# Reordering the side work of a hybrid decoder layer: attention of block B ahead of the recurrence's second half

## Chip, cores and metric

One core of a Trainium2 chip. The metric is the device time of one execution, in microseconds (us). TensorE is PE in the profile (PEld its weight loads), VectorE DVE, ScalarE ACT, GpSimd POOL, SyncE SP.

## What is computed

One layer of a decoder with two groups of heads, over 1024 prompt tokens and 8 sample tokens (each the next token of its own running sequence). Cut to what matters:

```python
def hybrid_layer(x, p, gla_fn, attn_fn, lambda_init):
    z = rmsnorm(x, p['norm_mix_g']) @ p['w_in']          # gq gk gv gg glr dq dk dv, 3088 columns
    log_a = log_sigmoid(glr @ p['w_gk2'] + p['b_gk']) / 16
    S_new, o_g = gla_fn(q_g, k_g, v_g, log_a)            # S_t = diag(a_t) S_{t-1} + k_t^T v_t, o_t = q_t S_t
    o_g = rmsnorm(o_g, p['gla_norm_g']) * silu(gg)
    o_d = attn_fn(rmsnorm(dq), rmsnorm(dk), dv, lam)     # softmax(q1 k1^T) - lam softmax(q2 k2^T), times v
    o_d = rmsnorm(o_d, p['diff_norm_g']) * (1.0 - lambda_init)
    x = x + concat(o_g, o_d) @ p['w_out']
    u = square(relu(rmsnorm(x, p['norm_ffn_g']) @ p['w_up']))
    return x + u @ p['w_down'], k_d, v_d, S_new
```

The prompt goes through the recurrence from a zero state and through causal attention. Each sample token has a state of its own and attends to 2048 cached positions (16 pages of 128, named by a page table) and to itself. All is fp32; the dense products are three fp32r matmuls each, of high and low parts (lines 85 to 87).

## The kernel before

**Blocks and the main line.** The tokens are two blocks: A, 512 tokens, and B, 512 and the 8 sample tokens. The main line of all engines is: `front` (the input projections, group by group: gv, low, gk, gq, dq, dk, dv, gg), then `feed_forward` for A, then for B. A feed forward is 8 output tiles of the mixing product ("out"), then 8 groups of 4 "up" tiles and 8 "down" tiles. Each weight tile is loaded by SP, split by ACT (high, L1982 and L1997) and DVE (low, L1986 and L2074). Block A's feed forward takes its results from two PSUM banks in turn; DVE frees one by an add (L2104, L2143) or by the scaled relu (L2125).

**Ticks.** The main line is cut into ticks of 12 dense matmuls: 104 in the front, 144 in a feed forward (an out or up tile is 2 ticks, a down tile 1). At each tick every engine calls the side jobs that `program` has put there by hand (`put(name, ticks)`) and each takes one step: a Python generator that issues a few instructions for that engine and yields. So the order within each engine's queue is fixed by this table; between engines only semaphores order. SP, which issues all DMAs, waits in its queue too.

**Side jobs of before** (ticks of the front by their number, of A's feed forward from 0): recurrence A (`recurA`), front; `attnA`, 40 steps at two a tick from front tick 79; `keysA`, front ticks 73 to 103; `mixA` from 96. Beside A's feed forward: `recurB` 0 to 34, `keysB` 0 to 66, `attnB` 33 to 72, `soft` 66 to 73, `values` 73 to 143, `sgla` 77 to 101 at every second, `mixload` 126, `mixB` from 137.

**The jobs.** `recurrence`: 4 chunks of 128 tokens, 8 steps each: subtract (DVE, L1114, L1116), exponentials (ACT, L1206 to L1209), keys and queries times decay (DVE, L1134 into `kp`, L1139 into `e`), then at the chunk's fifth step PE: transpose (L1254), levels (L1238), and later the products with values. `attention`: 16 units (4 heads, 4 query tiles), two steps each: scores on PE (L1412, L1415), maxima (DVE, L1537 or L1540), exponentials (ACT, L1468), mix of the two softmaxes (DVE, L1546 to L1548), transposes (PE, L1429), copies (ACT, L1478), product with the values (PE, L1443), its square and copy (ACT, L1482, L1488), the root of the head norm (POOL, L1519 to L1524), the scaling (ACT, L1493). `cached_keys`: per page a load of 256 KB, a product with the sample's query spread over the partitions (POOL, L2238), a reduction (DVE, L2226); block A's half of the 128 pages has 3 buffers and one for the query, B's half 4 and 2. `sample_softmax` works on all scores of the cached keys; `cached_values` loads two pages a step and multiplies them by coefficients laid out in `a_pad` (PE, L2443), after masks made by POOL (L2378 to L2382). `sample_recurrence` (`sgla`) updates the 8 states (PE, L2497; DVE, L2546) and reads them (PE, L2505). `mixing` turns the rows of both head groups for the mixing product (PE, L1640; DVE, L1663).

Buffers are given by hand at fixed places of SBUF, so a job that takes over a place first waits for the last reader (`region_free`, `sample_free`).

## Time and profile before

| | us |
|---|---|
| three runs | 1630.32, 1639.47, 1637.55 (median 1637.55) |
| profiled execution: time, span | 1636.6, 1634.7 |
| PE busy | 1465.6 (90%) |
| PE weight loads busy | 1182.6 (72%) |
| DVE busy | 852.0 (52%) |
| ACT busy | 531.1 (32%) |
| POOL busy | 316.6 (19%) |
| feed forward of A, first to last dense matmul | 491 to 1191 |
| feed forward of B | from 1192 |

The span is from the first to the last instruction; the execution's own time has some 2 us around it. A busy PE is not a PE at its peak: matmuls of 512 columns overlap, and their told length depends on the granted clock. Idle time before an instruction is put down to what ended it.

### The profile page before, as it was taken

Reading aid. Unit: us, or ns where it says so; the run is one execution under the profiler, and the core shown is the slowest. Engines: PE = TensorE matmul, PEld = TensorE weight load, DVE = VectorE, ACT = ScalarE, POOL = GpSimd, SP = SyncE. Lnnn points to the kernel's source line nnn. Section 1 sums busy time; section 2 is a strip of 40 time slices with the busy share of each in tenths; the row PEclk is TensorE's granted clock in tenths of the full one; section 3 lists DMA queues with packets and bytes.
Section 4 is the critical chain, followed back from the end, with each engine's and each line's share of the span. In section 5 each row is a group of like instructions: output and inputs, shape, how many; then the busy total and the mean of one; then the engine's idle time right before and its main releaser. Section 6 shows DMA issues by size and latency. Waiting matters only on the chain.

```text
span 1634.7 us, 23191 instructions
## 1 busy us (share of the span) xinstructions
PE 1465.6 (90%) x8649; PEld 1182.6 (72%) x8649; DVE 852.0 (52%) x1326; ACT 531.1 (32%) x964; POOL 316.6 (19%) x366
## 2 busy tenths in 40 slices
PE   7999988967778858789898999999989999999998
PEld 5787767745556646567676566565679999999998
DVE  4353565444556778565766433343435455554442
ACT  5462332223323342244543111121224233333222
POOL 2201222354563433233331000000012000000000
PEclk9999989978888878899998999999999999999999
DMA  7532231553345533534323556566423222322121
GB/s 247 157 98 87 59 100 59 177 153 109 116 147 175 178 126 123 196 99 130 123 90 109 181 174 189 178 221 218 141 93 129 103 103 104 104 104 91 66 77 54
DMA packets 115634, 211.99 MB, mean 130 GB/s; under 512 B 12665, under 2 KB 45722, under 8 KB 115522
## 3 DMA queue, kind: packets, MB, share of 16 engines
q1 hardware_dynamic: 115522, 210.50, 40.2%
q8 instruction: 69, 1.13, 0.3%
q14 instruction: 43, 0.35, 0.1%
HBM read 184.00 MB, written 26.46 MB: 129 GB/s over the span
## 4 chain that ended last, share of the span: by engine, by line
PE 56%; DVE 9%; ACT 4%; issue 3%; DMA 2%; POOL 2%; SPq 0%; ACTq 0%; POOLq 0%; DVEq 0%
PE ps L85 16%; PE ps L86 15%; PE ps L87 15%; PE ps L2443 4%; DVE uw_l L1986 2%; PE ps L1412 2%; POOL kr L2238 1%; PE ps L1238 1%; DMA kr<-in_cache_k 1%; ACT uw_h L1982 1%; DVE e L1114 1%; PE ps L1443 1%; DVE sd L2226 1%; DVE stat L1540 1%; DVE e L1139 1%
## 5 line engine op out<-in xcount | busy, mean ns | idle before, releaser
L85 PE MATMUL ps<-uh,dh 128*128 128x512 f32 (+2 forms) x768 | 253.9, 331 | 7.7 <-DVE xt L2143 7.7
L87 PE MATMUL ps<-uh,dl 128*128 128x512 f32 (+2 forms) x768 | 248.1, 323 | 0.0
L86 PE MATMUL ps<-ul,dh 128*128 128x512 f32 (+2 forms) x768 | 247.9, 323 | 0.0
L2238 POOL TENSOR_TENSOR kr<-kr,qb 128x512 f32<-128x512 f32 x128 | 174.8, 1375 | 160.1 <-DMA kr<-in_cache_k 119.7
L2143 DVE TENSOR_TENSOR xt<-xt,ps 128x256 f32<-128x256 f32 (+2 forms) x192 | 97.2, 511 | 179.8 <-PE ps L87 179.0
L85 PEld LDWEIGHTS ps<-uh,dh 128*128 128x128 f32 x768 | 146.4, 191 | 39.1 <-DVE xt L2143 19.8
L1982 ACT ACTIVATE uw_h<-raw_up 128x1024 fp32r<-128x1024 f32 x80 | 84.4, 1056 | 246.5 <-PE ps L87 246.5
L87 PEld LDWEIGHTS ps<-uh,dl 128*128 128x128 f32 x768 | 146.2, 190 | 12.1
L86 PEld LDWEIGHTS ps<-ul,dh 128*128 128x128 f32 x768 | 146.3, 191 | 9.8
L1997 ACT ACTIVATE dh<-raw_dn 128x1024 fp32r<-128x1024 f32 x64 | 67.0, 1047 | 261.2 <-PE ps L87 260.5
L85 PE MATMUL ps<-x2hB,uw_h 128*128 128x264 f32 (+1 forms) x512 | 145.9, 285 | 3.2 <-DVE uw_l L1986 2.6
L86 PE MATMUL ps<-x2lB,uw_h 128*128 128x264 f32 (+1 forms) x512 | 145.5, 284 | 0.0
L87 PE MATMUL ps<-x2hB,uw_l 128*128 128x264 f32 (+1 forms) x512 | 145.3, 284 | 0.0
L2226 DVE TENSOR_REDUCE sd<-kr 128x8 f32<-128x512 f32 x128 | 86.8, 679 | 79.3 <-POOL kr L2238 78.9
L1986 DVE TENSOR_TENSOR uw_l<-raw_up,uw_h 128x1024 fp32r<-128x1024 f32 x80 | 100.0, 1250 | 49.6 <-ACT uw_h L1982 49.6
L85 PE MATMUL ps<-x2hA,uw_h 128*128 128x512 f32 x256 | 110.9, 433 | 9.8 <-DVE uw_l L1986 9.8
L2125 DVE SCALAR_TENSOR_TENSOR xr<-ps,rb 128x256 f32<-128x256 f32 (+1 forms) x96 | 49.1, 514 | 116.1 <-PE ps L87 115.7
L86 PE MATMUL ps<-x2lA,uw_h 128*128 128x512 f32 x256 | 104.0, 406 | 0.0
L87 PE MATMUL ps<-x2hA,uw_l 128*128 128x512 f32 x256 | 103.6, 405 | 0.0
L2074 DVE TENSOR_TENSOR dl<-raw_dn,dh 128x1024 fp32r<-128x1024 f32 x64 | 81.2, 1268 | 37.7 <-ACT dh L1997 37.4
L85 PEld LDWEIGHTS ps<-x2hB,uw_h 128*128 128x128 f32 x512 | 97.3, 190 | 3.7 <-DVE uw_l L1986 2.8
L86 PEld LDWEIGHTS ps<-x2lB,uw_h 128*128 128x128 f32 x512 | 97.2, 190 | 0.0
(324 smaller groups left out, 2948.7 us busy)
## 6 DMA issues: line engine op xcount, KB each, us to landing
kr<-in_cache_k SPq DMA_DIRECT2D x128, 256.0 KB, 3.0
raw_up<-in_w_up_units SPq DMA_DIRECT2D x64, 512.0 KB, 3.7
raw_dn<-in_w_down SPq DMA_DIRECT2D x64, 512.0 KB, 4.6
vr<-in_cache_v SPq DMA_DIRECT2D x128, 256.0 KB, 3.1
raw<-in_w_in_units SPq DMA_DIRECT2D x24, 512.0 KB, 4.1
raw_up<-in_w_out_units SPq DMA_DIRECT2D x16, 512.0 KB, 3.8
xin<-in_x_prompt SPq DMA_DIRECT2D x8, 512.0 KB, 5.5
xt_scratch<-xts SPq DMA_DIRECT2D x8, 512.0 KB, 5.9
```

The source lines that it names most:

```text
L85: pe.matmul(out, lh, rh, start=first and n == 0, stop=False)
L86: pe.matmul(out, lh, rl, start=False, stop=False)
L87: ins = pe.matmul(out, ll, rh, start=False, stop=last and n == len(ks) - 1)
L1982: act.activation(uw_h[:, t % 2, :, :], raw_up[:, t % 2, :].rearrange("p (k c) -> p k c", c=P), ACT.Copy).then_inc(up_high, 1)
L1986: dve.tensor_tensor(uw_l[:, t % 2, :, :], raw_up[:, t % 2, :].rearrange("p (k c) -> p k c", c=P), uw_h[:, t % 2, :, :].bitcast(FP32), ALU. ...
L1997: act.activation(dh[:, x, :], raw_dn[:, x % 2, :], ACT.Copy).then_inc(dn_high, 1)
L2074: dve.tensor_tensor(dl[:, x, :], raw_dn[:, x % 2, :], dh[:, x, :].bitcast(FP32), ALU.subtract).then_inc(dn_low, 1)
L2125: dve.scalar_tensor_tensor(vt[:, i % 2, 0:spans[p][1]], ps[:, bank("up", g, x, p), 0:spans[p][1]], 0.0, rb2[:, tokens(p)], ALU.max, ALU.mu ...
L2143: dve.tensor_tensor(xt[:, o, c], xt[:, o, c], ps[:, bank("down", g, o, p), 0:spans[p][1]], ALU.add).then_inc(added, 1)
L2226: dve.tensor_reduce(m["sd"][:, b, g, :], ring[v % n_ring][:, :].rearrange("p (h d) -> p h d", d=DH), X, ALU.add).then_inc(k_used, 1)
L2238: pool.tensor_tensor(k[:, :], k[:, :], qb[b % len(qb)][:, :], ALU.mult).then_inc(k_multiplied, 1)
L2443: ins = pe.matmul(ps[32 * g:32 * g + 32, 6 + b % 2, :], a_pad[:, b % 2, 2 * l + j, :], vring[v % VRING][:, j, :], start=l < 2, stop=l >= 6 ...
```

## The change

The side jobs of A's feed forward stand in another order: `attnB` at ticks 0 to 42 (not at 17, in which the feed forward's norm uses a bank of the attention), 20 pages of `keysB` beside it at every second tick, the other 44 in ticks 43 to 68 with `sgla` at every second of 44 to 68, `soft` 68 to 75, `values` 75 to 143, `recurB` 71 to 105, `mixload` 108. The loads of `attnB` start in front tick 101. Cached keys have one query buffer, and 4 page buffers in block A, 3 and then 6 in block B; in block A the reduction comes a step later. The recurrence's keys and queries share one tile, `e`, and only the half of each level that is read is multiplied. In attention the root and the scaling come one step later. Banks and places change with it: values and softmax use banks 2 and 3, `sgla` 4 to 6, mixing B four banks; gg's tiles take the two banks in the other order. POOL fills `a_pad` and the mask once the coefficients are made, as `a_pad` takes the place of the scores. Cut to its core:

```diff
-        return g % 3 if GROUPS[g][0] not in ("dv", "gg") else GROUPS[g][1] % 2
+        kind, x = GROUPS[g]
+        return g % 3 if kind not in ("dv", "gg") else (x + (kind == "gg")) % 2
...
-            act.activation(tq[:, x % 2, :], ps[:, x % 2, :], ACT.Tanh, scale=m["hr"][:, x:x + 1]).then_inc(gate_soft, 1)
+            act.activation(tq[:, x % 2, :], ps[:, bank_of(START["gg"] + x), :], ACT.Tanh, scale=m["hr"][:, x:x + 1]).then_inc(gate_soft, 1)
...
-    g_in = at(f"g_in{part}", 166.625, [P, 3, 2, P])
-    gv = at(f"gv_in{part}", 169.625, [P, W])
-    e = at(f"e{part}", 171.625, [P, 9, 2, P])
-    kp = at(f"kp{part}", 180.625, [P, 8, 2, P])
-    at_sb = at(f"at_sb{part}", 188.625, [P, H, P])
-    kd = at(f"kd{part}", 190.625, [P, 2 * P])
+    base = (166.625, 178.625)[part]
+    g_in = at(f"g_in{part}", base, [P, 3, 2, P])
+    gv = at(f"gv_in{part}", base + 3, [P, W])
+    e = at(f"e{part}", base + 5, [P, 9, 2, P])
+    at_sb = at(f"at_sb{part}", base + 14, [P, H, P])
+    kd = at(f"kd{part}", base + 16, [P, 2 * P])
-    go = at(f"go{part}", 193.625, [P, W])
-    gate = at("gate1", 195.625, [P, W]) if part else None
+    go = at("go1", base + 17, [P, W]) if part else None
+    gate = at("gate1", base + 19, [P, W]) if part else None
...
-            eng.wait_ge(sem("product_made"), UNITS)
-            eng.wait_ge(sem("exped"), 2 * UNITS)
-            eng.wait_ge(sem("od_made"), UNITS)
-            eng.wait_ge(sem("mix_turned"), 8)
-            eng.wait_ge(sem("k_used"), KEY_PAGES)
+            eng.wait_ge(sem("product_made"), 2 * UNITS)
+            eng.wait_ge(sem("os_done"), 1)
+            eng.wait_ge(sem("state_stored"), 16)
...
+                dve.wait_ge(kd_turned, c)
...
-            dve.tensor_tensor(kp[:, :, :, :], e[:, 1:9, :, :], g_in[:, 1, :, :].unsqueeze(1).to_broadcast([P, 8, 2, P]),
-                              ALU.mult).then_inc(kq_made, 1)
+            k = g_in[:, 1, :, :]
+            dve.tensor_tensor(e[:, 8, :, :], e[:, 8, :, :], k, ALU.mult)
+            for l in range(1, 8):
+                v = side_of(e[:, l, :, :], l, 0)
+                ins = dve.tensor_tensor(v, v, side_of(k, l, 0), ALU.mult)
+            ins.then_inc(kq_made, 1)
...
-            dve.tensor_tensor(e[:, 0:8, :, :], e[:, 0:8, :, :], g_in[:, 0, :, :].unsqueeze(1).to_broadcast([P, 8, 2, P]),
-                              ALU.mult).then_inc(kq_made, 1)
+            q = g_in[:, 0, :, :]
+            dve.tensor_tensor(e[:, 0, :, :], e[:, 0, :, :], q, ALU.mult)
+            for l in range(1, 8):
+                v = side_of(e[:, l, :, :], l, 1)
+                ins = dve.tensor_tensor(v, v, side_of(q, l, 1), ALU.mult)
+            ins.then_inc(kq_made, 1)
...
-                        lhs = g_in[r, 1, t, :] if l == 0 else kp[r, l - 1, t, :]
+                        lhs = g_in[r, 1, t, :] if l == 0 else e[r, l, t, :]
...
-            pe.wait_ge(sem("exped"), 2 * UNITS)
-            pe.wait_ge(sem("p_copied"), UNITS)
-            pe.wait_ge(sem("od_made"), UNITS)
+            m["attend_banks_free"](pe)
+            pe.wait_ge(sem("os_done"), 1)
...
-ATTEND_STEPS = 2 * (UNITS + 4)
+ATTEND_STEPS = 2 * (UNITS + 5)
...
-        for x in ("o_summed", "state_summed", "s_updated", "go_made"):
-            eng.wait_ge(sem(x), CHUNKS * (part + 1))
-        if part:
-            eng.wait_ge(sem("og_gated"), NTILE)
-            eng.wait_ge(sem("go_out"), 64)
+        if part == 0:
+            for x in ("o_summed", "state_summed", "s_updated", "go_made"):
+                eng.wait_ge(sem(x), CHUNKS)
+        else:
+            eng.wait_ge(sem("product_made"), UNITS)
+            eng.wait_ge(sem("mix_turned"), 8)
+            eng.wait_ge(sem("k_used"), KEY_PAGES)
...
-        for x in ("o_summed", "state_summed", "go_made"):
-            sp.wait_ge(sem(x), CHUNKS * (part + 1))
-        sp.wait_ge(sem("level_picked"), 8 * CHUNKS * (part + 1))
-        m["kq_stored"](sp)
+        if part == 0:
+            for x in ("o_summed", "state_summed", "go_made"):
+                sp.wait_ge(sem(x), CHUNKS)
+            sp.wait_ge(sem("level_picked"), 8 * CHUNKS)
+            m["kq_stored"](sp)
+        else:
+            sp.wait_ge(sem("product_made"), UNITS)
         load_scored(sp, 0)
         load_scored(sp, 1)
         yield
         m["v_stored"](sp, part)
+        if part:
+            sp.wait_ge(sem("mix_turned"), 8)
         load_values(sp, 0)
...
-                pe.wait_ge(sem("rb2_made"), 1)
-                pe.wait_ge(sem("level_picked"), 8 * NTILE)
+                pe.wait_ge(sem("exped"), 2 * UNITS)
...
+            if part and n == NORM_UNIT and j == 1:
+                pe.wait_ge(sem("norm_step"), 1)
...
-                if 0 <= n - 4 < UNITS:
-                    normed(n - 4)
                 if 0 <= n - 3 < UNITS:
                     square(n - 3)
             else:
                 if 0 <= n - 2 < UNITS:
                     copy_turned(n - 2, 1)
+                if 0 <= n - 4 < UNITS:
+                    normed(n - 4)
             yield
 
...
-            u = n - 3
-            if j == 1 and 0 <= u < UNITS:
+            u = n - 4
+            if j == 0 and 0 <= u < UNITS:
...
-MIX_RING = 6
+MIX_RING = 8
+
+NORM_UNIT = 6
...
-        rowsB = at("rowsB", 192.625, [P, MIX_RING, W])
+        rowsB = at("rowsB", 178.625, [P, MIX_RING, W])
...
-    BANKS = 2 if part else 4
+    BANK0, BANKS = 2 + 2 * part, 4
...
-        return 7 - p if part else 2
+        return 7 - p if part else 6
...
-                pe.wait_ge(sem("mix_low"), 8)
+                pe.wait_ge(sem("p_copied"), UNITS + 2 * NORM_UNIT + 1)
...
+KEY_SLOTS = ((204.6875, 162.6875, 184.6875, 164.6875), (202.6875, 204.6875, 162.6875),
+             (166.625, 168.625, 170.625, 172.625, 174.625, 176.625))
+KEYS_BESIDE = 20
+
+
+def key_slots(v):
+
+    n = v - KEY_PAGES
+    return (0, 0) if n < 0 else (1, KEY_PAGES) if n < KEYS_BESIDE else (2, KEY_PAGES + KEYS_BESIDE)
...
+    LAG = 4 - part
+    STEPS = KEY_PAGES + LAG
...
+            if n:
+                sp.wait_ge(k_multiplied, PAGES * n)
+            sp.dma_start(qb[:, :], a["zq"][n].partition_broadcast(P)).then_inc(qb_in, 16)
...
+            v = first + s - 1
...
+            if s == 1 and part:
+                sp.wait_ge(sem("mix_turned"), 8)
+                sp.wait_ge(sem("k_used"), first)
+                load_query(0)
+            if first <= v < first + KEY_PAGES:
+                same = [x for x in range(v) if key_sem(x) == key_sem(v)]
+                if same:
+                    sp.wait_ge(k_used, same[-1] + 1)
+                if v == KEY_PAGES + KEYS_BESIDE:
+                    sp.wait_ge(sem("product_made"), 2 * UNITS)
+                page = sp.value_load(m["pages"][0:1, v:v + 1], min_val=0, max_val=NPOOL - 1)
+                sp.dma_start(place(v)[:, :], a["cache_k"][bass.ds(page, 1), :, :].rearrange("a p n -> p (a n)"))\
+                    .then_inc(page_in[key_sem(v)], 16)
+            n = s - 2
+            if n > 0 and n % PAGES == 0 and n < KEY_PAGES:
+                load_query(n // PAGES)
...
+            v = first + s - LAG
...
-    a_pad = at("a_pad", 182.625, [P, 2, PAGES, 32])
-    hmask = at("hmask", 186.625, [P, W])
-    vm = at("vm", 188.625, [P, W])
+    a_pad = at("a_pad", 9.75, [P, 2, PAGES, 32])
+    hmask = at("hmask", 1.5, [P, W])
+    vm = at("vm", 162.6875, [P, W])
...
+        sp.wait_ge(sem("product_made"), 2 * UNITS)
+        sp.wait_ge(sem("k_used"), 2 * KEY_PAGES)
...
-        pool.wait_ge(sem("p_turned"), 3 * UNITS)
+        pool.wait_ge(sem("coef_made"), 1)
+        pool.wait_ge(sem("k_multiplied"), 2 * KEY_PAGES)
...
-                        pe.wait_ge(v_masked, b - 1)
+                        pe.wait_ge(v_added, b)
...
-                    ins = pe.matmul(ps[32 * g:32 * g + 32, 6 + b % 2, :], a_pad[:, b % 2, 2 * l + j, :],
+                    ins = pe.matmul(ps[32 * g:32 * g + 32, 2 + b % 2, :], a_pad[:, b % 2, 2 * l + j, :],
...
-    st_new = at("st_new", 192.625, [P, NS, 2, P])
+    st_new = at("st_new", 178.625, [P, NS, 2, P])
...
-                    ins = pe.matmul(ps[:, 2 + x % 2, t * 2 * DV:(t + 1) * 2 * DV], k_alone[x // 4][:, x % 4, t * P:(t + 1) * P],
+                    ins = pe.matmul(ps[:, 5 + x % 2, t * 2 * DV:(t + 1) * 2 * DV], k_alone[x // 4][:, x % 4, t * P:(t + 1) * P],
...
-        put("keysA", [t0 + 31 * i // (KEY_PAGES + 3) for i in range(KEY_PAGES + 3)])
+        put("keysA", [t0 + 31 * i // (KEY_PAGES + 4) for i in range(KEY_PAGES + 4)])
         t0 = TICK[START["gg"]]
+        put("loadB", [t0 + 14])
         put("mixA", [t0 + 9, t0 + 10, t0 + 11, t0 + 12] + [t0 + 13 + i // 2 for i in range(7)])
         t0 = FRONT_TICKS
-        put("recurB", range(t0, t0 + side["recurB"]["steps"]))
-        t1 = t0 + side["recurB"]["steps"] - 2
-        put("loadB", [t1, t1 + 2])
-        put("attnB", [t1] + [t1 + 1 + i for i in range(ATTEND_STEPS - 1)])
-        put("keysB", range(t0, t0 + KEY_PAGES + 3))
-        t1 += 33
+        put("loadB", [t0 + 1])
+        norm = 2 * KT + 1
+        put("attnB", [t0 + i for i in range(ATTEND_STEPS + 1) if i != norm])
+        late = t0 + ATTEND_STEPS + 1
+        put("keysB", [t0 + 2 * (i + 1) for i in range(KEYS_BESIDE)])
+        put("keysB", [late + 25 * i // (KEY_PAGES + 3 - KEYS_BESIDE) for i in range(KEY_PAGES + 3 - KEYS_BESIDE)])
+        put("sgla", range(late + 1, late + 1 + 26, 2))
+        t1 = late + 25
         put("soft", [t1 + i for i in (0, 1, 3, 4, 5, 6, 7)])
         put("values", range(t1 + 7, t0 + FEED_TICKS))
-        put("sgla", range(t1 + 11, t1 + 11 + 26, 2))
-        put("mixload", [t0 + 126])
+        put("recurB", range(t1 + 3, t1 + 3 + side["recurB"]["steps"]))
+        put("mixload", [t1 + 40])
         put("mixB", [t0 + 137 + i // 2 for i in range(9)])
 
         def run(e, eng):
...
-            for name in ("attnB", "soft", "sgla", "values", "mixB"):
+            for name in ("values", "mixB"):
```

Left out are further places of tiles and bank numbers of the same kinds.

## Rows read from the trace of the kernel before

**Rows 1.** Stretches: length; busy us of PE, PEld, DVE, ACT, POOL; clock; DMA share, GB/s.

```profile
320.00:491.00 171.00, 120.05 (x544) 86.68 (x544) 86.05 (x149) 54.12 (x172) 95.52 (x107) 0.84 0.44 131
491.00:670.00 179.00, 140.49 (x771) 112.40 (x772) 131.74 (x185) 57.60 (x94) 67.14 (x48) 0.85 0.45 144
670.00:865.00 195.00, 168.19 (x866) 126.02 (x865) 130.71 (x174) 85.90 (x188) 64.19 (x76) 0.95 0.39 126
865.00:898.00 33.00, 26.30 (x107) 20.78 (x106) 18.59 (x30) 11.06 (x23) 6.00 (x11) 0.84 0.42 134
898.00:1192.00 294.00, 291.15 (x1239) 176.95 (x1237) 119.75 (x167) 56.76 (x74) 2.54 (x4) 0.99 0.57 181
```

**Rows 2.** Timeline of PE, 472 to 481: start, length, instruction.

```profile
473.15 0.63 PE L85 MATMUL ps<-wh,xhB 128*128 128x512 f32 x1
473.58 0.63 PE L86 MATMUL ps<-wl,xhB 128*128 128x512 f32 x1
...
480.63 0.39 PE L86 MATMUL ps<-wl,xhB 128*128 128x512 f32 x1
480.86 0.40 PE L87 MATMUL ps<-wh,xlB 128*128 128x512 f32 x1
```

**Rows 3.** Groups by line, 320 to 491: count, busy us, mean ns, idle before.

```profile
L2238 POOL TENSOR_TENSOR kr<-kr,qb 128x512 f32<-128x512 f32 x59 | 74.6, 1277 | 37.0 <-DMA kr<-in_cache_k 36.8
L2226 DVE TENSOR_REDUCE sd<-kr 128x8 f32<-128x512 f32 x59 | 40.4, 684 | 65.5 <-POOL kr L2238 65.3
...
L86 PE MATMUL ps<-wl,xhB 128*128 128x512 f32 x56 | 24.5, 437 | 0.0
```

**Rows 4.** Waits, 320 to 491: who for whom, us in total, times, longest.

```profile
DVE sd L2226 <- POOL kr L2238: 65.3, 39, 4.9
POOL oss L1522 <- ACT ps L1482: 36.9, 13, 8.1
...
PE ps L1443 <- ACT od L1488: 17.8, 7, 5.4
...
PE ps L85 <- DVE zs L769: 10.8, 1, 10.8
```

**Rows 5.** Waits, 491 to 670.

```profile
PE ps L1238 <- DVE e L1139: 16.5, 3, 8.1
...
PE ps L85 <- DVE uw_l L1986: 11.3, 2, 9.8
...
PE ps L1254 <- DVE kp L1134: 4.7, 3, 2.7
```

**Rows 6.** Timeline of DVE, 627 to 637.

```profile
629.75 5.66 DVE L1114 TENSOR_TENSOR e<-g_in 128x256 f32<-128x256 f32 x7
635.33 0.41 DVE L1116 TENSOR_TENSOR e<-g_in 128x256 f32<-128x256 f32 x1
```

**Rows 7.** Waits, 670 to 865.

```profile
PE ps L1429 <- ACT attn_t L1478: 12.6, 6, 3.3
...
PE ps L1412 <- DMA qt<-kept_qt: 5.9, 1, 5.9
```

**Rows 8.** The chain that ended last, 670 to 865: attention B's first and last scores.

```profile
678.64 2.51 PE ps L1412 x8
...
844.80 1.92 PE ps L1412 x8
```

**Rows 9.** Groups by line, 670 to 865.

```profile
L1986 DVE TENSOR_TENSOR uw_l<-raw_up,uw_h 128x1024 fp32r<-128x1024 f32 x10 | 13.9, 1394 | 8.5 <-ACT uw_h L1982 8.5
```

**Rows 10.** Groups by line, 898 to 1192.

```profile
L1986 DVE TENSOR_TENSOR uw_l<-raw_up,uw_h 128x1024 fp32r<-128x1024 f32 x16 | 19.6, 1225 | 5.8 <-ACT uw_h L1982 5.8
...
L2497 PE MATMUL ps<-zs,k_alone 8*128 8x256 f32 x32 | 8.0, 387 | 0.0
L2505 PE MATMUL ps<-st_new,q 128*8 128x128 f32 x64 | 7.2, 272 | 0.0
```

**Rows 11.** Timeline of POOL, 871 to 880.

```profile
875.80 3.32 POOL L2382 TENSOR_SCALAR_AFFINE_SELECT hmask<-hmask 128x512 f32<-128x512 f32 x4
```

More of the change, by code:

```diff
@@ L1605, in load @@
         for u in range(MIX_RING):
-            load_unit_rows(sp, u)
+            t, half = tiles[u]
+            sp.dma_start(rowsB[:, u, :], a[("og", "od_scratch")[half]][HALF + t * P:HALF + (t + 1) * P, :])\
+                .then_inc(b_in, 16)
         yield
-    def load_unit_rows(sp, u):
-        t, half = tiles[u]
-        sp.dma_start(rowsB[:, u % MIX_RING, :], a[("og", "od_scratch")[half]][HALF + t * P:HALF + (t + 1) * P, :])\
-            .then_inc(b_in[u // MIX_RING], 16)
-    def sync(sp):
-        for s in range(STEPS):
-            if part and s == 3:
-                for u in range(MIX_RING, 8):
-                    sp.wait_ge(turned, before + u - MIX_RING + 1)
-                    load_unit_rows(sp, u)
-            yield
     def tensor(pe):
@@ new lines, in sync @@
+            if s == 1 and part == 0:
+                last_scale(sp)
+                sp.wait_ge(sem("kv_stored"), 32)
+                m["kq_stored"](sp)
+                for x in ("o_summed", "state_summed", "s_updated", "go_made"):
+                    sp.wait_ge(sem(x), CHUNKS)
+                load_query(0)
+            if s == 1 and part:
[11 more added lines that the diff above has]
+                    .then_inc(page_in[key_sem(v)], 16)
```

171 lines of the change are left out of this document (77 added, 94 removed).

## The prediction

> **What bounds the kernel now.** I read the stretches first, then who waits for whom in each. The PE row of the page hides what matters here: its 90% is a mean over stretches with different limits [rows 1]. From 898 to 1192, with the cached values beside the feed forward, PE is busy 291.2 of 294 us: nothing can be won there but PE work itself. In the four stretches before it, PE idles 51.0, 38.5, 26.8 and 6.7 us, together 123. After an idle stretch matmuls run at half clock for a while: a 512-column matmul then starts 0.43 us after the last, against 0.23 at full clock, and is told as 0.63 us long against 0.39 [rows 2]. A mean of 437 ns [rows 3] says that a fifth ran at half clock from 320 to 491; of the 264 dense ones that is some 55 times 0.2 = 11 us. I spread this by the granted clock (0.16, 0.15, 0.05 and 0.16 below full, times the length of each stretch): 11, 11, 4 and 2, together 28 us. So some 150 us between 320 and 898 are neither PE work nor speed. The PE instructions of the change are the ones of before in another order, so only these 150 can move. The sum below is against the profiled execution, 1636.6 us (span 1634.7), 1 us under the median.
>
> The unit of the schedule, a tick, is 12 dense matmuls: 12 times 0.23 = 2.8 us at full clock. The feed forward has 144.
>
> **Front, 320 to 491.** PE waits there for ACT's copy of attention A's result and for a sample row of the projection [rows 4]. Both stand behind one knot: DVE idles 65.3 us in 39 waits for POOL's key products; POOL idles 36.9 for ACT's square [rows 4] and 36.8 for pages [rows 3]; ACT is fed by DVE. The change touches it in four places: a fourth page buffer; one more step between POOL and DVE (LAG 4); the roots one step later on POOL, the scaling one on ACT; gg's banks swapped, so that its first tile takes the bank that came free a tile earlier. A page takes 171/59 = 2.9 us now; four buffers for three make 2.2 of that if the round trip is all of it, and POOL's own floor is 1.28 [rows 3]. The three query reloads stay. The sample row's 10.8 I take down to 4, since what is left is DVE's own backlog; the other 40 of idle I take to about 22, and clock with them (11 to 6). Of 62 I keep 32: **-30**. Bounds: -45 if only POOL's floor held, -10 if only the bank swap counted.
>
> **Recurrence B.** It sat beside the first 35 ticks; there PE waits 16.5 and 4.7 us for its products and 11.3 for low weights, most of it at the feed forward's norm [rows 5]. Its chain (subtract, exp, keys, queries) lasts longer than the four ticks of 2.8 us that it is given. One set of seven subtractions takes 5.66 us with POOL beside it, where one alone takes 0.41 [rows 6]. It moves beside the values: 294 us for 70 ticks, 4.2 a tick, DVE busy 120 and POOL 2.5 [rows 1]. The four chunks waited 21 plus some 6 of slow clock; I keep 5: **-22**. Its narrower products (8 instructions for 1, half the columns) I cost at **-3** for the eight chunks; +3 if each small one carries more overhead than it saves. The added wait for the keys' transpose is over long before. Queued behind recurrence B's waits on SP is the values' loading; the state that it waits for was sent 7 ticks before, some 20 us.
>
> **Attention B** moves from ticks 33-72 to 0-42. Its scores waited 5.9 for qt, its turned blocks 12.6 for ACT's copies [rows 7]. Its first loads, 1.5 MB, now go out in the front's last ticks beside key pages (hidden by them; +4 there if not): -6. Its pace was (844.80 - 678.64)/15 = 11.1 us a unit [rows 8], of which 5.7 is dense work. An up tile has two weight splits of 1.22 on DVE [rows 10] and two half as wide, some 3.8 us; an out tile one less, 3. So I take the same pace, with fewer keys beside it: -3. The norm, for which attention leaves out tick 17, no longer stands behind a set of subtractions: -5. The sample row before the first out tile: -3, as that tile takes the other bank. Together **-17**.
>
> **Keys B.** 20 pages beside attention, then 44 in 25 ticks with the sample recurrence: 25 times 2.8, and 8.0 + 7.2 us of that recurrence's PE work [rows 10], is 85 us. POOL needs 44 times 1.28 [rows 3] = 56 and two query reloads that nothing hides now, 4 to 5 each: 66, below 85, with six buffers. On DVE an up tile has its 3.8 and 3.8 pages at 0.68 [rows 3], 6.4 for 5.7 of PE, and the sample recurrence's adds. I take **+10** (0 if the down ticks catch it up, +28 by the first rival).
>
> **Softmax, fill, mixing.** The softmax keeps its 6.7 of idle [rows 1]. New: POOL clears a_pad and builds hmask only after the coefficients; the last part alone is 3.32 us [rows 11], the whole some 5. DVE waits for it at its first value step, and its adds for the down tiles are queued behind; PE's two banks cover 5.6. The recurrence's first chunk stands in that queue too: **+6**. Mixing B has four banks for two (-2), but the sample result is due two ticks later (+3): **+1**.
>
> **Sum:** -30 -22 -3 -17 +10 +6 +1 = -55, so 1581.6; the recurrence A chain before 320 may give 1.5 more beside the stretches read here: **1580**.
>
> **A rule weighed.** The row first: DVE's split of weights takes 1394 ns with POOL busy a third of the time [rows 9], and 1225 with it idle [rows 10], 0.17 us more on the mean. The Trainium skill (SBUF — State Buffer, section SBUF: two separate sides) says that a GpSimd instruction and a VectorE one with two SBUF inputs take turns at a shared port pair, each for its whole length. Rows 6, 9 and 10 agree in direction; no row shows how often they meet.
>
> **Rivals.**
> 1. *Keys stay at the front's pace* (20%). SP issues pages in order behind the weights. At 2.9 us a page 44 take 128 us, where I have 95: +33, less what the down ticks catch up, some +28: **1608**. For: the waits of rows 4. Against: six buffers, and no roots beside.
> 2. *Exclusive turns* (8%). If pages and DVE's two-input instructions never overlapped, an up tile would need 3.8 times 1.28 plus 3.1 (two splits at 1.22, one of 0.65) = 8.0 us for 5.7. Six such tiles: +14: **1594**. For: the 5.66 of rows 6. Against: only 1394 for 1225. This is what the Trainium skill's rule on the port pair would do here, held to the letter.
> 3. *Attention loses its cover* (9%), slower than before. It now starts with the out tiles, whose banks DVE frees by an add; in DVE's queue stands the mix, which waits for ACT, which waits for PE's turned block. In its stretch a unit has 7.4 us of DVE's time and 4.9 of ACT's (130.7 and 85.9 over 17.6 units [rows 1]); with all of it behind the 5.7 of dense work a unit would take 18, with most of it 16, for 11. Place: the units from tick 1 to the second down phase, 13: +65: **1645**. Over all sixteen it decides from 57/16 = 3.6 us a unit on.
> 4. *Nothing moves* (8%). Each wait taken away is taken over by the next in DVE's queue, which has nearly the same work in it: **1637**, give or take 6.
>
> **How the numbers follow.** Forecast 55%, rivals 20, 8, 9 and 8. A measurement here tells about 0.5% (8 us) from no change. Forecast and rivals 1 and 2 end faster, 0.83, less 0.01 for rival 1's upper end; same 0.09, slower 0.09. Range: down to the front at -45, the keys at 0 and ten more from the waits of attention B (1545); up past rival 1 to where rival 4 begins (1622). It leaves out rivals 3 and 4 and a little more.
>
> **What would show it.** Right: DVE's wait for POOL's keys in the front under 35 us; no wait of PE over 3 us for the recurrence's queries; attention's scores 11 us apart or less; the keys' 25 ticks within 100 us; a granted clock of 0.9 or more from 320 on. Wrong: DVE waits for POOL in the keys' ticks (rival 1), weight splits of 1.6 us and more (rival 2), PE waits for ACT's copies or for DVE's adds in the out ticks (rival 3). The forecast fails as a whole if the front's stretch stays over 160 us.

## The result, and the profile after

The changed kernel takes 1594.2 us (median of 4 runs, 1590.33 to 1599.75), the kernel before 1636.98 in the same comparison: a ratio of 0.9747, 95% interval 0.9703 to 0.9792. That is 43 us less; 57 were forecast, and the range (1545 to 1622) holds the result. The profiled execution of after is the longest of its four (1599.75, span 1598.0), which matters below.

Stretches of the changed kernel, cut where its stages end (columns as in [rows 1]):

```profile
320.00:457.00 137.00, 107.46 (x526) 77.94 (x526) 87.58 (x144) 52.88 (x169) 88.83 (x103) 0.94 0.49 151
457.00:678.00 221.00, 199.19 (x992) 150.39 (x991) 138.40 (x174) 105.69 (x223) 62.60 (x76) 0.94 0.38 128
678.00:795.00 117.00, 95.55 (x401) 73.94 (x400) 76.99 (x106) 17.08 (x21) 62.48 (x44) 0.88 0.51 167
795.00:842.00 47.00, 28.68 (x95) 22.00 (x94) 31.94 (x58) 13.96 (x16) 2.69 (x4) 0.75 0.31 112
842.00:1151.00 309.00, 302.51 (x1495) 190.08 (x1493) 150.68 (x277) 73.97 (x118) 10.09 (x15) 0.99 0.55 180
```

The stages are: 320 the front's end, 457 attention B with 20 key pages, 678 the other 44 pages with the sample recurrence, 795 the softmax, 842 cached values with the recurrence's second half, 1151 block B's feed forward. PE idles 29.5, 21.8, 21.5, 18.3 and 6.5 us in the five from 320 to 1151, 98 in all; it was 126 from 320 to 1192 [rows 1]. A's feed forward starts at 457.3, where it started at 491.1. That is no fair mark, since PE waits for the sample row right before 491.1 in the kernel before (6.2 us) and behind its first tick in this one (4.5). By the start of the third tick, 498.8 before and 471.0 now, 28 us are won. From there to its last matmul it takes 679.6 us for 692.3: 13 more. Behind it the profiled execution gives 4 back (447.4 for 443.6).

The waits of the changed kernel in the front, which answer to the knot of [rows 4], DVE's and then PE's (us in total, times, longest):

```profile
DVE sd L2265 <- POOL kr L2277: 21.5, 17, 3.4
```

```profile
PE ps L1466 <- ACT od L1511: 15.2, 7, 6.5
...
PE ps L1450 <- DVE p0a L1571: 5.7, 3, 4.2
PE ps L85 <- DVE wl L729: 1.9, 1, 1.9
```

DVE's wait for POOL's key products fell from 65.3 us in 39 to 21.5 in 17, and the 10.8 for the sample row is gone (1.9, for something else). The wait for ACT's copy of attention A's result is nearly what it was, 15.2 for 17.8.

The waits of all engines in the key ticks, 678 to 795, the stage that did not do as forecast:

```profile
POOL kr L2277 <- DMA kr<-in_cache_k: 25.4, 11, 7.1
POOL kr L2277 <- DMA qb<-kept_zq: 18.0, 2, 14.5
...
DVE sd L2265 <- POOL kr L2277: 15.3, 10, 5.5
...
PE ps L85 <- DVE xt L2159: 10.6, 1, 10.6
...
PE ps L85 <- DVE dl L2090: 6.5, 1, 6.5
...
PE ps L2539 <- DVE st_new L2588: 4.3, 1, 4.3
```

Behind them stand two places. First, DVE's timeline around 694 (start, us, instruction, how many):

```profile
694.03 3.43 DVE L2566 TENSOR_TENSOR k_alone<-kq_g,ident 8x1024 f32<-8x1024 f32 x2
697.39 4.89 DVE L2573 COPY q<-gbs 64x8 f32<-64x8 f32 x4
702.31 0.69 DVE L2159 TENSOR_TENSOR xt<-xt,ps 128x512 f32<-128x512 f32 x1
```

The four copies L2573 move 8 numbers a partition, 0.17 us each in the kernel before (0.155 to 0.173), and take 1.2 each here; PE's 10.6 us end with the add behind them, at 702.3. POOL multiplies eight pages without a pause meanwhile, and the single records go in step: the copies end at 698.61, 699.84, 701.06 and 702.28, each 0.03 us after the end of a page's product (698.59, 699.81, 701.03, 702.25). Second, from 709 POOL stands still; POOL's timeline, then SP's issues, and what SP waited for between 700 and 726:

```profile
690.43 11.82 POOL L2277 TENSOR_TENSOR kr<-kr,qb 128x512 f32<-128x512 f32 x8 [3.17 <-DMA kr<-in_cache_k]
...
723.81 2.48 POOL L2277 TENSOR_TENSOR kr<-kr,qb 128x512 f32<-128x512 f32 x2 [14.51 <-DMA qb<-kept_zq]
```

```profile
704.34 1.45 SPq L2252 DMA_DIRECT2D kr<-in_cache_k  x2
717.22 0.34 SPq L1793 DMA_DIRECT2D raw_up<-in_w_up_units  x1
717.61 0.43 SPq L1805 DMA_DIRECT2D raw_dn<-in_w_down  x1
719.13 0.36 SPq L2252 DMA_DIRECT2D kr<-in_cache_k  x1
719.54 0.42 SPq L2230 DMA_DIRECT2D qb<-kept_zq  x1
720.74 1.46 SPq L2252 DMA_DIRECT2D kr<-in_cache_k  x2
```

```profile
SPq L1793 <- DVE uw_l L2002: 11.4, 1, 11.4
```

The page multiplied at 723.8 needed the next sample's query row. SP sent its load only at 719.5: in SP's queue it stood behind two weight loads (717.2, 717.6) whose buffers had to come free. PE's waits in the other stages, 457 to 678, 795 to 842 and 842 to 1151:

```profile
PE ps L1450 <- ACT attn_t L1501: 9.5, 6, 2.7
PE ps L85 <- DVE zs L770: 4.5, 1, 4.5
PE ps L1429 <- ACT p1b L1491: 3.3, 1, 3.3
```

```profile
PE ps L2301 <- DVE small L2332: 9.0, 1, 9.0
PE ps L2309 <- DVE small L2349: 6.0, 1, 6.0
PE ps L2305 <- DVE small L2338: 3.3, 1, 3.3
```

```profile
PE ps L85 <- DVE xt L2159: 6.3, 1, 6.3
```

No wait of PE for a product of the recurrence's second half is left: in the old first ticks it had 21.2 us [rows 5]. What is left of its cost is the 6.3 us just shown: before that add, DVE waits 4.0 us for ACT's part of a weight split, which stands behind two of the recurrence's exponentials of 1.9 us each. The softmax has 18.3 of PE's waits for three DVE results, where the kernel before had 6.5 in the softmax's ticks and 2.7 for attention's copy.

### The profile page after: what moved, and what is told of

The parts are those of the page before. It is cut to its first block, busy times and chain, and to the rows that moved or that the text cites. A ratio compares the mean times of both kernels' runs of the same rounds, so it can differ in the third digit from the quotient of the medians.

```text
span 1598.0 us, 23302 instructions
## 1 busy us (share of the span) xinstructions
PE 1456.0 (91%) x8649; PEld 1176.5 (74%) x8649; DVE 850.0 (53%) x1438; ACT 530.1 (33%) x964; POOL 313.9 (20%) x366
## 4 chain that ended last, share of the span: by engine, by line
PE 55%; DVE 8%; issue 5%; DMA 3%; ACT 3%; POOL 2%; SPq 1%; ACTq 0%; POOLq 0%; DVEq 0%
PE ps L85 16%; PE ps L87 15%; PE ps L86 15%; PE ps L2486 4%; DMA kr<-in_cache_k 2%; POOL kr L2277 1%; PE ps L1429 1%; DVE uw_l L2002 1%; PE ps L1250 1%; PE ps L1466 1%; DVE sd L2265 1%; ACT uw_h L1998 1%; DMA out_y_prompt<-y 1%; PE ps L1450 1%; DVE stat L1563 1%
## 5 line engine op out<-in xcount | busy, mean ns | idle before, releaser
L2277 POOL TENSOR_TENSOR kr<-kr,qb 128x512 f32<-128x512 f32 x128 | 170.7, 1354 | 151.1 <-DMA kr<-in_cache_k 104.6
L86 PE MATMUL ps<-x2lB,uw_h 128*128 128x264 f32 (+1 forms) x512 | 144.7, 283 | 0.0
L85 PE MATMUL ps<-x2hA,uw_h 128*128 128x512 f32 x256 | 111.1, 434 | 10.6 <-DVE xt L2159 10.6
```

Source lines behind the costliest of these rows:

```text
L85: pe.matmul(out, lh, rh, start=first and n == 0, stop=False)
L86: pe.matmul(out, lh, rl, start=False, stop=False)
L2277: pool.tensor_tensor(k[:, :], k[:, :], qb[:, :], ALU.mult).then_inc(k_multiplied, 1)
```

## The experiments

All ratios are to the kernel before, with their 95% intervals. The changed kernel stands at 0.9747. A difference of two ratios times 1637 is what one kernel has over another. Most intervals are 4 us to either side, the changed kernel's is 7: a difference to the changed kernel is uncertain by some 8 us, one between two others by some 6. So a small difference rests on what the traces show beside it. A wait "in tick 47" lies between that tick's twelve matmuls and the next tick's first.

**What made the front's gain.** Three runs undo one part of the changed kernel each; one makes the front's edits, all but the roots', on the kernel before.

e1_bank:

```diff
     def bank_of(g):
         kind, x = GROUPS[g]
-        return g % 3 if kind not in ("dv", "gg") else (x + (kind == "gg")) % 2
+        return g % 3 if kind not in ("dv", "gg") else x % 2
```

> The changed kernel with the bank swap of the gate tiles undone (gg's first tile again takes the bank of dv's last). Theory 1, each repair of the front has its own share: PE's wait of about 10.9 us for the first gate tile comes back (it is 1.9 in the changed kernel), the time goes from 1594 to about 1602, ratio to before 0.979. Theory 2, it was only DVE's backlog and the wait moves elsewhere: ratio 0.975, within 2 us of 1594, and the waits of the other tiles shrink by as much.

Measured: 1599.59 us, ratio 0.9761 (0.9738 to 0.9785): 2 us more by the ratios, 5 by the medians. PE's waits for the sample row, from 320 to 480:

```profile
PE ps L85 <- DVE zs L770: 16.5, 2, 8.4
```

The sample row's wait is back, 16.5 us in two: 8.4 in the front, and 8.1 right before the feed forward's first matmul, where the changed kernel has 4.5 a tick later. By the third tick it is 4.5 us behind the changed kernel (475.5 for 471.0), and by the ninth 4.4. So the swap is worth 2 to 5 us, under half of the 12 us of waits that it takes away: between the two theories.

e2_slots3:

```diff
-KEY_SLOTS = ((204.6875, 162.6875, 184.6875, 164.6875), ...
+KEY_SLOTS = ((204.6875, 162.6875, 184.6875), ...
...
-    LAG = 4 - part
+    LAG = 3
...
-        put("keysA", [t0 + 31 * i // (KEY_PAGES + 4) for i in range(KEY_PAGES + 4)])
+        put("keysA", [t0 + 31 * i // (KEY_PAGES + 3) for i in range(KEY_PAGES + 3)])
```

> The changed kernel with block A's cached keys back at three buffers and three steps between load and sum. Theory 1 (the page's round trip held the front, what the prediction leaned on): DVE's wait for POOL's key products in the front goes from 21.5 us back to 50 or more, the front loses 15 to 25 us, time about 1614, ratio 0.986. Theory 2 (it was the roots' order on POOL): DVE's wait rises by less than 15 us, time under 1600, ratio 0.977.

Measured: 1610.77 us, ratio 0.984 (0.9816 to 0.9863), 15 us more; the third tick starts at 487.6, 16.6 later. DVE's waits for POOL in its front:

```profile
DVE sd L2265 <- POOL kr L2277: 41.8, 26, 4.9
```

41.8 us of waits for POOL against 21.5: under the 50 that I had put for theory 1, but the time is theory 1's, at its lower end. The fourth buffer with its longer distance is the largest single part; which of these two carries it was not run apart.

e3_roots puts POOL's root and ACT's scaling back to one step earlier (the later stages keep their ticks); POOL's part of the edit:

```diff
-            u = n - 4
-            if j == 0 and 0 <= u < UNITS:
+            u = n - 3
+            if j == 1 and 0 <= u < UNITS:
                 x, e, total = oss[:, u % 4:u % 4 + 1], stat[:, u % 4, 7:8], stat[:, u % 4, 0:1]
```

> The changed kernel with attention's roots on POOL and the scaling on ACT back at one step earlier (the places of the later stages are kept). Theory 1 (the buffers alone made the gain): POOL's wait for ACT's square comes back (37 us in the front before) but PE hardly sees it, time within 3 us of 1594, ratio 0.975 to 0.977. Theory 2 (POOL's in-order wait for the square held the key products behind it, and DVE behind them): DVE's wait for POOL in the front rises from 21.5 to over 40 us, time 1602 to 1612, ratio 0.98 to 0.985.

Measured: 1596.22 us, ratio 0.9745 (0.9719 to 0.9771), no difference. POOL's wait for ACT's square comes back at 16.5 us, not at 36.9, and DVE's waits for POOL stay at 23.4. The third tick even starts 4.2 us earlier (466.8), but attention B's ticks 8 to 42 take 181.2 us for 174.8. Theory 1 held: this part of the change, which I had counted among four, carries nothing that these runs can tell. The edit puts both blocks' attention back, and in its trace the two places pull against each other.

b2_front, on the kernel before: the bank swap, the fourth buffer and LAG 4 as above, with block A's attention moved by 64 bytes to make room.

> The kernel before with the front's edits alone, without the roots' step: the fourth page buffer of block A's keys, one more step to DVE, and gg's banks swapped. Theory 1 (the front's gain stands by itself): the feed forward starts 30 to 38 us earlier than 491, the time is 1600 to 1606, ratio 0.978 to 0.981, so that the rest of the change brings only some 10. Theory 2 (the gain needs the later stages, or is given back at the feed forward's start): the front ends 30 us earlier but the time falls by under 20, ratio over 0.988.

Measured: 1607.55 us, ratio 0.9813 (0.9789 to 0.9837), 31 us less than before. The third tick starts at 464.1, 34.7 earlier, and 5 of that are gone by the ninth (502.0 for 531.5): between them PE waits 5.4 us for recurrence B and 3.5 for a low weight split. So the front's gain stands by itself, and all the rest of the change, with six jobs moved, brings 11 by the ratios, 13 by the medians, give or take 8. The parts that e1_bank and e2_slots3 undo come to 17 to 20 us of the front's 28 to 31; the rest needs the swap and the buffers together, or is noise, and no run tells which.

**The narrower products.** b1_narrow, on the kernel before:

```diff
-            dve.tensor_tensor(e[:, 0:8, :, :], e[:, 0:8, :, :], g_in[:, 0, :, :].unsqueeze(1).to_broadcast([P, 8, 2, P]),
-                              ALU.mult).then_inc(kq_made, 1)
+            q = g_in[:, 0, :, :]
+            dve.tensor_tensor(e[:, 0, :, :], e[:, 0, :, :], q, ALU.mult)
+            for l in range(1, 8):
+                v = side_of(e[:, l, :, :], l, 1)
+                ins = dve.tensor_tensor(v, v, side_of(q, l, 1), ALU.mult)
+            ins.then_inc(kq_made, 1)
```

(and the keys in the same way, into `e` instead of `kp`)

> The kernel before with nothing but the narrower products of the recurrence (the multiplied keys written over e, eight instructions of half the columns for one wide one). Theory 1 (the prediction's term of 3 us for eight chunks): 1634, ratio 0.998. Theory 2 (each product is shorter by 0.4 to 1.4 us as in the changed kernel, and in the first 320 us and from 491 to 590 PE waits for them, so it is worth more): 8 to 10 us, ratio 0.994 to 0.995. Theory 3 (hidden): 1.000.

Measured: 1636.45 us over 12 runs, ratio 0.999 (0.9974 to 1.0005): 1.6 us less, 4.3 less to 0.8 more. Theory 1's 3 us are within that, and so is theory 3's nothing; theory 2's 8 to 10 are not. In the changed kernel a set of narrow products takes 1.83 us all eight times, where the wide one took 2.28 to 3.35. In this run thirteen of the sixteen sets do so too, but three of the four query sets beside the feed forward take 3.96, 5.04 and 5.13 us, longer than the wide products that they replace (2.28, 3.35 and 2.75). The second of these three, DVE's timeline and then POOL's:

```profile
602.25 1.49 DVE L1149 TENSOR_TENSOR e<-e,g_in 128x256 f32<-128x256 f32 x1
603.66 3.63 DVE L1152 TENSOR_TENSOR e<-e,g_in 128x128 f32<-128x128 f32 x7
```

```profile
601.99 4.14 POOL L2251 TENSOR_TENSOR kr<-kr,qb 128x512 f32<-128x512 f32 x3 [23.52 <-DMA qb<-kept_zq]
```

POOL's three products end at 603.45, 604.86 and 606.12, and three of DVE's eight end 0.15 to 0.29 us later (603.73, 605.00, 606.27), at 1.35 to 1.49 us each; the others take 0.28. In the fourth query set, at 507, it is POOL's page that takes 3.89 us, and DVE's eight take their 1.83. PE's waits in the first stage beside the feed forward:

```profile
PE ps L1251 <- DVE e L1152: 18.1, 3, 8.9
PE ps L85 <- DVE uw_l L1999: 12.9, 3, 9.8
```

18.1 us, where 16.5 stood: cutting one product into eight shortens a set by 0.4 us and more where POOL leaves it alone, and lengthened three by 1.7 to 2.4 where pages come in turn with its pieces. So this run prices the narrow products in the old order. In the changed kernel, where recurrence B stands beside a POOL that is all but idle, no run has them apart.

**Why the rest brought only 11.** e4_query starts from the changed kernel; each later one says from which.

e4_query, a second buffer for the query row of the third sample of the late pages (block B had two query buffers before the change):

```diff
+    qb6 = at("qb6", 162.6875, [P, W]) if part else None
...
-            if n:
+            if n == 6:
+                sp.wait_ge(k_used, 82)
+            elif n == 7:
+                sp.wait_ge(k_multiplied, 97)
+            elif n:
                 sp.wait_ge(k_multiplied, PAGES * n)
...
-            if n > 0 and n % PAGES == 0 and n < KEY_PAGES:
+            if n > 0 and n % PAGES == 0 and n < KEY_PAGES and not (part and n > PAGES):
                 load_query(n // PAGES)
+            if v in (84, 100):
+                load_query(2 if v == 84 else 3)
```

> The changed kernel with a second buffer for block B's third query row, so that the last two query loads are sent 12 pages ahead instead of when POOL needs them. Theory 1 (the 14.5 us of idle on POOL at 709 to 724, behind SP's weight loads, cost PE its waits of 4.3 and 6.5 us and more in the ticks 50 to 58): the gap falls under 4 us, the 25 key ticks from 116.7 to about 108, time 1586, ratio 0.970. Theory 2 (DVE's own work in these ticks is the bound, and POOL only catches up): the gap goes, the 25 ticks stay at 114 or more, time 1593, ratio 0.974.

Measured: 1586.84 us, ratio 0.9697 (0.9668 to 0.9725), 8 us less than the changed kernel; the 25 key ticks take 108.6 us for 116.7. PE's waits in them:

```profile
PE ps L85 <- DVE xt L2159: 10.9, 1, 10.9
PE ps L85 <- DVE dl L2090: 8.3, 1, 8.3
```

Theory 1: the wait of 4.3 us for the state's adds is gone, and so is POOL's 14.5 for a query. It also shows how one execution differs from the next: attention's ticks 0 to 42, in which nothing differs, take 214.0 us for 220.9, at a granted clock of 0.98 for 0.94 in that stretch. The ratios and medians are what the 8 us go by, and they are no more than their uncertainty; what bears them out is that the key ticks take 114.6 to 116.7 us in all four traces without this edit (the changed kernel's, e1_bank, e2_slots3, e3_roots).

e5_q4act, e4_query with the four small copies on ACT:

```diff
-                st.note(dve.tensor_copy(diag, gbs[r, 0, t, :]))
...
+        act.wait_ge(k_alone_made, 2)
+        for t in range(2):
+            for hf in range(2):
+                r = rows[hf]
+                diag = q4[:, :, :, :, :].rearrange("p t h b c -> p t h (b c)")[r, t, hf, 0:64:9]
+                act.activation(diag, gbs[r, 0, t, :], ACT.Copy).then_inc(sem("gbs_made"), 1)
```

> The kernel of e4_query with the sample recurrence's four small copies of queries (8 elements a partition each) moved from DVE to ACT. On DVE they took 4.89 us for four while POOL multiplied eight pages without a pause, 0.76 in the kernel before. Theory 1 (DVE's small copies each wait for a whole POOL page, and this delays the add that PE waits for 10.9 us at in tick 47): on ACT the four take under 1.5 us beside the same pages, PE's wait there falls to about 6, time 1582 to 1583, ratio to e4_query 0.997. Theory 2 (the copies are slow on any engine, from their strided output): they take 4 us or more on ACT too.

Measured: 1585.92 us, ratio 0.9691 (0.9668 to 0.9713). By itself 1 us is no difference, and theory 1's time is missed by 3. In its trace, though, PE's wait in tick 47 falls from 10.9 to 6.1 us and the key ticks from 108.6 to 104.6, as theory 1 has it; e10_both below tries the copies once more. ACT's timeline, and POOL's at the same time:

```profile
690.80 0.93 ACT L2539 ACTIVATE q<-gbs 64x8 f32<-64x8 f32 x4 [22.09 <-DVE k_alone L2584]
```

```profile
683.75 17.41 POOL L2287 TENSOR_TENSOR kr<-kr,qb 128x512 f32<-128x512 f32 x10 [3.05 <-DMA kr<-in_cache_k]
```

Four copies in 0.93 us on ACT beside a POOL that runs on, 4.89 on DVE. The copies are not slow in themselves: it is DVE beside POOL. With the ends in step shown above this is the exclusive turn of my second rival, at an instruction that I had not thought of. The Trainium skill (SBUF — State Buffer, section Who interferes with whom) lists VectorE's copy among the operations that can take the port pair shared with GpSimd, and says that the second one then waits for the whole instruction of the first; 1.2 us a copy beside products of 1.26 us agrees. The same section says that on trn2 a reduction never meets it, and DVE's reductions of the pages did take 0.67 to 0.69 us in all 128 places, beside POOL as elsewhere.

e6_lag, e4_query with the late pages loaded a step earlier ahead of POOL, and summed two steps behind it:

```diff
-    LAG = 4 - part
-    STEPS = KEY_PAGES + LAG
+    LATE = KEY_PAGES + KEYS_BESIDE
+    STEPS = KEY_PAGES + (5 if part else 4)
+
+    def made_at(v):
+        return v - first + (2 if v < LATE else 3)
+
+    def summed_at(v):
+        return v - first + (4 if part == 0 else 3 if v < LATE else 5)
```

> The kernel of e4_query with a longer distance for the late pages of block B's keys: POOL multiplies two steps after SP sends the load instead of one, DVE sums two steps after that instead of one. Theory 1 (SP's order behind the weight loads makes pages late, and DVE in its turn waits 8.5 us in 8 for POOL and is then late for the split that PE waits 8.3 us for in tick 55): DVE's waits fall under 3 us, PE's wait in tick 55 under 3, time 1580 to 1582. Theory 2 (the bound is DVE's own work, four sums and four state adds in front of the split): the wait of tick 55 stays over 6 us, time within 2 us of e4_query's 1586.8.

Measured: 1578.78 us, ratio 0.9651 (0.9626 to 0.9676), 7.5 us less than e4_query; the key ticks take 101.4. PE's waits in them, then DVE's:

```profile
PE ps L85 <- DVE dl L2090: 5.8, 1, 5.8
PE ps L85 <- DVE xt L2159: 4.8, 1, 4.8
```

```profile
DVE sd L2280 <- POOL kr L2291: 0.8, 2, 0.5
```

The time and DVE's waits (8.5 to 0.8) are theory 1's. The wait for the split in tick 55 fell only from 8.3 to 5.8, not under 3, so part of it is DVE's own work, as theory 2 has it. The wait in tick 47 fell from 10.9 to 4.8, although the four copies take 4.92 us there too: the sums in front of them no longer wait for pages. The edit moves two distances at once. POOL's own waits for pages hardly change (34.5 us in 15 in e4_query, 32.5 in 17 here), so what its 7.5 us buy is that DVE no longer stands behind a late page; what the earlier load alone would bring was not run.

e10_both, e6_lag with e5_q4act's copies (the base that the next three are read against):

> The kernel of e6_lag with e5_q4act's copies on ACT and nothing else: the base of e7_soft, which had both and the respaced softmax. The key ticks took 101.4 us in e6_lag and 97.1 in e7_soft. Theory 1 (the copies are worth their 4 us also here, and the respaced softmax gave its part back): about 1575, ratio 0.9625 to 0.963, and the key ticks 97 to 98 us. Theory 2 (they are hidden once the pages come late, and the spacing neither gained nor lost): 1578 to 1580, ratio 0.965, the key ticks over 100 us.

Measured: 1575.09 us over 6 runs, ratio 0.961 (0.9583 to 0.9637), under e6_lag by 4 us by the medians and 7 by the ratios; the key ticks take 96.1 for 101.4. That stretch, and PE's waits in it:

```profile
678.00:774.00 96.00, 90.58 (x400) 70.31 (x399) 72.98 (x102) 18.13 (x25) 66.80 (x45) 0.95 0.65 206
```

```profile
PE ps L85 <- DVE dl L2090: 3.9, 1, 3.9
PE ps L2560 <- DVE st_new L2605: 1.5, 1, 1.5
```

Theory 1. The wait of tick 47 is gone altogether. This is the fastest kernel of the study, 19 us under the changed one by the medians and 22 by the ratios, outside both intervals; its PE idles 5.4 us in the key ticks against 21.4.

e7_soft, e10_both with the softmax spaced out:

```diff
-        put("soft", [t1 + i for i in (0, 1, 3, 4, 5, 6, 7)])
-        put("values", range(t1 + 7, t0 + FEED_TICKS))
+        put("soft", [t1 + i for i in (0, 3, 5, 6, 8, 9, 10)])
+        put("values", sorted(list(range(t1 + 11, t0 + FEED_TICKS)) + [t0 + i for i in (93, 109, 125)]))
```

> The kernel of e6_lag with e5_q4act's copies on ACT, and the softmax of the cached scores given ten ticks for seven (its PE steps three, two and three ticks behind the DVE steps they need, the values' steps start four ticks later and catch up by three doubled steps in down ticks). Theory 1 (PE's three waits of 7.2, 3.3 and 7.3 us in ticks 69, 71 and 73 come from PE being sent there before DVE's queue can be done): they fall under 6 us in sum, 10 to 12 us less; with 1 us for the copies the time is 1566 to 1569, ratio 0.958. Theory 2 (DVE's queue in these ticks is itself the bound and the waits reappear as waits for its splits or adds): under 4 us less, 1575 or more.

Measured: 1579.87 us, ratio 0.9658 (0.9634 to 0.9682), slower than e10_both by 8 us by the ratios and 5 by the medians (their intervals overlap by 0.0003). PE's waits in the softmax's ticks, and from there to the end:

```profile
PE ps L2319 <- DVE small L2352: 6.6, 1, 6.6
PE ps L85 <- DVE dl L2090: 4.4, 1, 4.4
PE ps L85 <- DVE uw_l L2002: 2.1, 1, 2.1
PE ps L2323 <- DVE small L2363: 1.3, 1, 1.3
```

```profile
PE ps L2487 <- DVE vm L2479: 5.0, 1, 5.0
PE ps L1656 <- DVE zs L2472: 4.7, 1, 4.7
...
PE ps L2500 <- DMA vr<-in_cache_v: 2.3, 1, 2.3
```

17.8 us of softmax waits became 7.9, as theory 1 wanted, and 6.5 us of waits for DVE's splits are new; then the values' doubled steps make PE wait for a page (2.3) and for the mask's product (5.0), and the sample's result comes later into block B's mix (4.7 for 1.9). The feed forward takes 670.2 us for e10_both's 670.4, the part behind it 450.7 for 445.3. Theory 2 has the time (over 1575), and part of the place: 6.5 us reappear as waits for splits. The rest went to the far end, which neither theory had.

e8_rec, e7_soft with `recurB` at t1 + 12 and `mixload` at t1 + 49:

> The kernel of e7_soft with the recurrence's second half started nine ticks later, behind the softmax, where in the changed kernel its first chunk's subtractions, exponentials and products stand in DVE's queue during the softmax (about 7 us of DVE). Theory 1 (the first chunk in the queue costs PE what the prediction put down, some 3 of its 6 us): 3 to 4 us less than e7_soft. Theory 2 (after the spacing DVE has the time): within 1.5 us of e7_soft. Theory 3 (its end meets the mix of block B): slower by 2 us or more.

Measured: 1578.31 us, ratio 0.9645 (0.9617 to 0.9672), within 2 us of e7_soft, which can't be told from theory 1's 3 to 4 or theory 2's 1.5. The softmax's eleven ticks 68 to 78 fall from 58.9 to 41.3 us, and the 29 after them rise from 144.7 to 157.6, the last 36 from 149.8 to 152.7: the work is moved, not hidden. In those 29 PE waits 8.9 us for DVE's adds and 5.9 for loads of values, where e7_soft has 3.1 and 2.3 from its softmax on.

e9_even, e8_rec with unequal shares of pages (three in an up tick to five in a down tick):

> The kernel of e8_rec with the late key pages spread by what DVE has to do for the feed forward: three shares in an up tick and five in a down tick, where they had equal shares. Theory 1 (PE's wait of 5.8 us for the low split in tick 55 comes from four sums and four state adds in front of it): that wait falls under 3 us, the time 2 to 4 us under e8_rec. Theory 2 (POOL then falls behind in the down ticks, 1.28 us a page and 2.8 a tick, and DVE waits for it): DVE's waits for POOL rise over 5 us and nothing is gained.

Measured: 1582.69 us, ratio 0.9686 (0.9659 to 0.9712), 7 us slower than e8_rec by the ratios, 4 by the medians. DVE's waits for POOL in the key ticks come back (6.5 us in 5) and so does PE's wait of tick 47 (6.2); the one of tick 55, which was to fall under 3, is 4.6 for e8_rec's 3.9. Theory 2.

## Why the prediction was right or wrong

Term by term, from the profiled executions, with the third tick's start as the front's end. "Beyond" is what a stretch takes beyond 2.83 us a tick and PE's side work: idle time and slow clock.

| term | forecast | measured |
|---|---|---|
| front, with recurrence A | -31.5 | -28 (498.8 to 471.0) |
| recurrence B, attention B, narrower products in B | -40.5 | -53: beyond 78.1 in ticks 2 to 65 before; 21.8 in ticks 2 to 42 now, and 3.5 more beside the values |
| keys B with the sample recurrence | +10 | +30: beyond 30.1 in 25 ticks |
| softmax, fill, first chunk | +6 | +10: beyond 14.7 before, 24.4 now |
| mixing tail, with all behind A's feed forward | +1 | +4 |
| sum | -55 | -37 (1634.7 to 1598.0) |

The medians give -43: the profiled execution of the changed kernel was its longest. The time fell inside the range and nearer the forecast than its parts did, and that is luck in part: the stage of attention and recurrence brought 12 more than forecast and the keys 20 less. That the result is also rival 2's 1594 is chance: its sum was turns in six up tiles, and turns are not what most of the loss came from.

**Front: right, for its main reason.** b2_front has 31 us less than before, and the wait for POOL that was to fall under 35 is 21.5. Of the causes the buffer with its distance is worth 15, the bank swap 2 to 5, the roots nothing that can be told; 8 to 14 us are in none of them singly.

**Recurrence B and attention B: more than forecast, and not separable by these runs.** No wait of PE for the recurrence's products is left, of 21.2; beside the values it causes one of 6.3, by its exponentials ahead of a weight split in ACT's queue, where I had left it 5. qt's 5.9 us are gone as said. The norm's stall (9.8 at once) is gone as well, for which I had 5. Attention keeps its pace, (636.36 - 469.63)/15 = 11.1 us a unit from its first scores to its last; the 3 us for fewer keys beside it don't show.

**Narrower products, -3 for all eight chunks:** b1_narrow has 1.6, and anything from 4.3 less to 0.8 more. Beside the term stood "+3 if each small one carries more overhead than it saves". The cost is real but is no overhead of each: it comes where a small product meets POOL's pages. The order of the change takes it away, and there the -3 was not tested.

**Keys B, +10: wrong by 20, and the step that failed.** The 85 us of PE's own time in these ticks stands (70.8 and 15.9 of side work); they took 116.7. In my sum stood "two query reloads that nothing hides now, 4 to 5 each: 66, below 85". A reload was priced by its transfer, and the pages, with six buffers, at no wait at all. What counts is when SP gets to send, and SP stood behind weight loads: one reload left POOL idle for 14.5 us, the other for 3.5, and POOL waited another 25.4 us for pages, so that DVE waited 15.3 for POOL. e4_query takes 8 us back and e6_lag 7.5. So the mechanism of rival 1 (SP in order behind the weights) was real. It is shown for the query load; for the pages it is the likely cause of what e6_lag mends by more distance. Together they cost some 15 us of its 28, at single places and not as an even 2.9 us a page. The last 4 to 7 are the copies on DVE (e10_both against e6_lag: 4 by the medians, 7 by the ratios, 5 in the key ticks), rival 2's mechanism, for which I had counted splits of weights and not small copies. The splits show it too: the five of down weights in these ticks have a mean of 1.59 us, where splits with no page beside them have a median of 1.22, and the five of up weights 1.29. With all three mended the ticks take 96.1, where the forecast had 95.

**Softmax, fill and first chunk, +6:** the fill was right, 5.6 us on POOL, of which DVE waits 2.3 and PE none. The rest are the softmax's own three waits, 18.3 for 6.5, and in DVE's timeline the last sums and the sample recurrence's last step now stand in front of it. Not all of it is DVE's work: before the third wait ends, DVE itself waits 5.3 us for ACT's part of a weight split, which stands behind two exponentials of the recurrence's first chunk (1.9 us each). e7_soft and e8_rec show that this isn't to be had by spacing alone.

**Rivals 3 and 4.** In the out ticks PE waits for attention 3.3 us at once at most, so its cover held. Rival 4 has small places: over half of the bank swap's wait and all of what the softmax's spacing took away came back elsewhere. The granted clock from 320 to 1151 was 0.94, 0.94, 0.88, 0.75 and 0.99, where 0.9 or more was to be seen; the two below it are the two stages that went over their terms. Of the range, the upper end was to lie where rival 4 begins; by that rival's own "give or take 6" this is 1631 and not 1622, on which nothing hangs here.

## What to carry to other kernels

Price a reload by when its queue can send it, not by its transfer: a load that must wait for its own buffer, in a queue that also feeds the main line, stalls by the main line's rhythm, and one more buffer is worth more than its bytes look. When jobs are rearranged, look at what small instructions of VectorE come to stand beside long ones of GpSimd, for a copy of eight numbers a partition can cost 1.2 us there, and one product cut into eight can take longer than the whole. And a stall taken out of a fixed order counts only by the time of the whole program: the softmax's stage became 7.6 us shorter by its spacing (66.5 to 58.9), and the program no faster.

## What was not expected of the hardware

- Four DVE copies of 8 numbers a partition took 1.18 to 1.22 us each beside POOL's uninterrupted products, 0.155 to 0.173 alone; on ACT, beside the same products, 0.21 to 0.22.
- Of two DVE products with two SBUF inputs of 8 x 1024 numbers one took 1.23 us and one 2.27 beside the same POOL products, both 1.21 in the kernel before; reductions of 128 x 512 took 0.65 to 0.69 in both.
- DVE products of 128 x 128 numbers took 0.28 us in the changed kernel and up to 1.38 beside POOL's pages in b1_narrow.
- One kernel's executions on one chip spread by 9 us (1583.78 to 1592.48 for e4_query), with the same instructions at a granted clock of 0.958 to 0.964 over the span.
